# The last chunk's down projection in two token parts of 192 and 128 columns, with the final norm and the stores made per part

## The reference

```
def conv_ffn(h, buf, w_up, conv_w, conv_b, w_down):
    T = h.shape[1]
    z = h @ w_up
    a, v = z[..., :D_FF], z[..., D_FF:]
    ...
    hid = jax.nn.silu(conv) * v
    return hid @ w_down, ext[:, -(CONV_W - 1):]
...
    f, new_conv = conv_ffn(rmsnorm(x, norm_ffn_g), conv_buf, w_up, conv_w, conv_b, w_down)
    x = x + f
...
y = xf * lax.rsqrt(jnp.mean(xf * xf, axis=-1, keepdims=True) + EPS)
return (y * g.astype(jnp.float32)).astype(x.dtype)
```

## Time and profile before

| what | value |
|---|---|
| three runs | 2090.78, 2099.86, 2101.64 us, median 2099.86 |
| profiled execution | 2091.91 us, its span 2090.1 us |
| PE busy | 2017.1 us (97%), 13394 matmuls and as many weight loads |
| DVE, ACT busy | 1089.1 us (52%), 746.9 us (36%) |
| mean granted TensorE clock | 0.98 of full speed |

### The profile page before, as it was taken

How to read it: one execution, slowest core, us unless ns; L and a number is a source line. 1 busy time by engine, 2 the same in 40 slices (tenths; PEclk the granted TensorE clock), 3 DMA queues, 4 the chain that set the end, 5 groups by cost and what they waited for, 6 DMA issues and landing times.

```text
span 2090.1 us, 34134 instructions
## 1 busy us (share of the span) xinstructions
PE 2017.1 (97%) x13394; PEld 1958.9 (94%) x13394; DVE 1089.1 (52%) x1454; ACT 746.9 (36%) x810; POOL 55.6 (3%) x180
## 2 busy tenths in 40 slices
PE   7999999999999799999898999999999999999996
PEld 7999999999986688999898999999999999999996
DVE  6854344434336444145455656556556555555557
ACT  5356542332245443133243332333233233232332
POOL 0010000000000000000000000000000000000000
PEclk9999999999999899799999999999999999999998
DMA  6434444444450477334443434434443443433432
GB/s 226 151 140 147 159 142 159 140 155 147 145 217 21 150 244 259 134 141 154 161 157 128 150 139 155 148 141 153 148 153 140 150 151 140 149 148 144 158 143 98
DMA packets 58168, 318.16 MB, mean 152 GB/s; under 512 B 6466, under 2 KB 6658, under 8 KB 25090
## 3 DMA queue, kind: packets, MB, share of 16 engines
q1 hardware_dynamic: 57458, 313.15, 41.9%
q10 hardware_dynamic: 656, 4.27, 0.5%
HBM read 313.08 MB, written 4.32 MB: 152 GB/s over the span
## 4 chain that ended last, share of the span: by engine, by line
PE 93%; DVE 2%; ACT 1%; issue 1%; DMA 1%; SPq 0%; POOL 0%; ACTq 0%; DVEq 0%; POOLq 0%
PE ps L1118 93%; ACT w_hi L423 1%; DMA xT<-in_x 0%; PE ps L1375 0%; DVE x L1111 0%; PE ps L1288 0%; DVE x L707 0%; DVE w_lo L707 0%; DVE pool_ta L707 0%; DVE h_lo L783 0%; DMA c_raw<-in_cache 0%; PE ps L1308 0%; DVE norm_tmp L707 0%; DVE pool_tb L707 0%; POOL ql_lo L389 0%
## 5 line engine op out<-in xcount | busy, mean ns | idle before, releaser
L707 DVE TENSOR_TENSOR w_lo<-w_raw,w_hi 128x2048 fp32r<-128x2048 f32 (+1 forms) x267 | 609.7, 2284 | 496.2 <-ACT w_hi L423 495.9
L1118 PE MATMUL ps<-h_hi,w_hi 128*128 128x320 f32 x2512 | 746.6, 310 | 30.5 <-ACT w_hi L423 10.7
L423 ACT ACTIVATE w_hi<-w_raw 128x2048 fp32r<-128x2048 f32 (+1 forms) x267 | 508.3, 1905 | 700.6 <-PE ps L1118 694.3
L1118 PE MATMUL ps<-h_lo,w_hi 128*128 128x320 f32 x2512 | 744.5, 310 | 0.9 <-DVE h_lo L783 0.9
L1118 PEld LDWEIGHTS ps<-h_hi,w_hi 128*128 128x128 f32 x2512 | 475.5, 189 | 34.4 <-issue 13.4
L1118 PEld LDWEIGHTS ps<-h_lo,w_hi 128*128 128x128 f32 x2512 | 474.5, 189 | 1.9 <-DVE h_lo L783 1.6
L1118 PE MATMUL ps<-h_hi,w_lo 128*128 128x320 f32 x2512 | 393.6, 308 | 0.0
L1118 PEld LDWEIGHTS ps<-h_hi,w_lo 128*128 128x128 f32 x2512 | 374.9, 187 | 0.0
L1118 PE MATMUL ps<-hid_hi,w_hi 128*128 128x320 f32 x704 | 216.7, 308 | 0.0
L1118 PE MATMUL ps<-hid_lo,w_hi 128*128 128x320 f32 x704 | 216.6, 308 | 0.0
L1118 PE MATMUL ps<-hid_hi,w_lo 128*128 128x320 f32 x704 | 216.6, 308 | 0.0
(11 more groups left out here) (197 smaller groups left out, 1769.1 us busy)
## 6 DMA issues: line engine op xcount, KB each, us to landing
w_raw<-in_slabs SPq DMA_DIRECT2D x253, 1024.0 KB, 4.8
w_raw<-in_cache_t SPq DMA_DIRECT2D x64, 288.0 KB, 3.6
c_raw<-in_cache SPq DMA_DIRECT2D x64, 256.0 KB, 3.7
w_whole<-in_slabs SPq DMA_DIRECT2D x4, 1024.0 KB, 5.9
xT<-in_x SPq DMA_DIRECT2D x4, 640.0 KB, 8.4
x_again<-in_x ACTq DMA_DIRECT2D x1, 2560.0 KB, 11.4
out_y<-x SPq DMA_DIRECT2D x4, 640.0 KB, 2.9
w_raw<-in_slabs SPq DMA_DIRECT2D x2, 512.0 KB, 7.1
```

Of the source, the lines that this page charges most:

```text
L423: return nc.scalar.activation(out, in_, ACT.Copy)
L707: return nc.vector.tensor_tensor(out, a, b, op)
L1118: return nc.tensor.matmul(out, a, b, start=start, stop=stop, **kw)
```

## The change

The last chunk's down projection is taken out of `chunk` and written as `end_part(p, d)`. The tokens are cut in two parts, p = 0 with columns 0 to 191 and p = 1 with columns 192 to 319. First all four slabs are multiplied with part 0, then all four with part 1. For that all four split slabs have to stay: d = 0 and 1 in `w_hi`, `w_lo`, and d = 2 and 3 in new buffers `end_hi`, `end_lo` that lie where `h2_hi`, `h2_lo` lay. The normal loop now ends one chunk earlier on PE, and the up projection of the last chunk is written out.

```
+PARTS = ((0, 192), (192, T))
...
+        def end_tile(p, k):
+
+            d, n = k // 4, k % 4
+            width = PARTS[p][1] - PARTS[p][0]
+            high = d < 2 if p == 0 else d % 2 == 0
+            return ps[:, 4 * high + n, 0:width]
+
+        def end_sum_of(p):
+
+            return ps[:, 3 + p, 0:PARTS[p][1] - PARTS[p][0]]
...
+            for p, (c0, c1) in enumerate(PARTS):
+                for k in range(4):
+                    sp.wait_ge(y_step[p], k + 1)
+                    sp.dma_start(y[:, 4 * k:4 * k + 4, c0:c1], yg[:, 4 * k:4 * k + 4, c0:c1]).then_inc(out_sem, 16)
...
+            def end_tiles(p, k0, k1):
+
+                c0, c1 = PARTS[p]
+                for k in range(k0, k1):
+                    act.wait_ge(end_taken[p], k + 1)
+                    nc.scalar.activation(sq[:, k, c0:c1], x1[:, k, c0:c1], ACT.Square).then_inc(end_sq[p], 1)
+                    nc.scalar.activation(yg[:, k, c0:c1], x1[:, k, c0:c1], ACT.Copy, scale=col("g_fin", k)
+                                         ).then_inc(end_gain[p], 1)
...
+            def end_slab(d, g):
+
+                if d < 2:
+                    act.wait_ge(raw_full[d], 16 * ((raw_index(g) + 2) // 2 + 1))
+                    if d == 0:
+                        act.wait_ge(slab_used, G0["ffn"] + 12 * NCH - 4)
+                    copy(end_hi[d][:, :], raw[d]).then_inc(hi_ready, 1)
+                end_tiles(0, 4 * d, 4 * d + 4)
...
+            def end_add(p, d):
+
+                c0, c1 = PARTS[p]
+                for k in range(4 * d, 4 * d + 4):
+                    dve.wait_ge(end_done[p], k + 1)
+                    tt(x1[:, k, c0:c1], end_tile(p, k), x1[:, k, c0:c1], ALU.add).then_inc(end_taken[p], 1)
+
+            def end_squares(p, d):
+
+                c0, c1 = PARTS[p]
+                dve.wait_ge(end_sq[p], 4 * d + 4)
+                if d > 1:
+                    dve.wait_ge(end_added[p], d - 1)
+                tt(sq[:, 0:4, c0:c1], sq[:, 0:4, c0:c1], sq[:, 4 * d:4 * d + 4, c0:c1], ALU.add).then_inc(end_added[p], 1)
...
+            def end_scale(p, d):
+
+                c0, c1 = PARTS[p]
+                part = yg[:, 4 * d:4 * d + 4, c0:c1]
+                dve.wait_ge(end_gain[p], 4 * d + 4)
+                tt(part, part, rstd[:, None, c0:c1].to_broadcast([P, 4, c1 - c0]), ALU.mult).then_inc(y_step[p], 1)
+
+            def end_low(d):
+
+                dve.wait_ge(hi_ready, G0["ffn"] + 12 * NCH - 2 + d + 1 - NWHOLE)
+                tt(end_lo[d][:, :], raw[d], end_hi[d][:, :], ALU.subtract).then_inc(lo_ready, 1)
...
-            sum_squares(3, KD)
+            chunk(NCH - 1, last_chunk=True)
+
+            def end_part(p, d):
+
+                c0, c1 = PARTS[p]
+                whi, wlo = (w_hi[d], w_lo[d]) if d < 2 else (end_hi[d - 2], end_lo[d - 2])
...
+                order = ([(n, k) for k in range(FPC) for n in range(4)] if p == 0 and d == 0 else
+                         [(n, k) for n in range(4) for k in range(FPC)])
+                for n, k in order:
...
+                    if k == 0:
+                        if p == 0 and d % 2:
+                            pe.wait_ge(end_taken[0], 4 * (d - 1) + n + 1)
+                        if p and d < 2:
+                            pe.wait_ge(end_taken[0], 4 * (2 * d + 1) + n + 1)
+                        if p and d == 1 and n == 3:
+                            pe.wait_ge(end_norm[0], 1)
+                        if p and d >= 2:
+                            pe.wait_ge(end_taken[1], 4 * (d - 2) + n + 1)
+                    out = end_tile(p, 4 * d + n)
+                    w = 4 * n + k
+                    mm(out, blk(whi, w), hid_hi[:, k, c0:c1], k == 0, False)
+                    mm(out, blk(whi, w), hid_lo[:, k, c0:c1], False, False)
+                    last = mm(out, blk(wlo, w), hid_hi[:, k, c0:c1], False, k == FPC - 1)
+                    if k == FPC - 1:
+                        last.then_inc(end_done[p], 1)
...
+            for d in range(4):
+                end_part(0, d)
+            end_part(1, 0)
+            end_total(0)
+            for d in range(1, 4):
+                end_part(1, d)
+            end_total(1)
```

More of the change, by code:

```diff
@@ L202, in program @@
         cstate = sb("cstate", [P, FT, 1 + NB, CW - 1], at=b_reg + 12288)
+        end_hi = [sb(f"end_hi{s}", [P, SLAB], F32R, at=r1 + s * SLAB * 4) for s in range(2)]
+        end_lo = [sb(f"end_lo{s}", [P, SLAB], F32R, at=r1 + (2 + s) * SLAB * 4) for s in range(2)]
+        yg = sb("y_gain", [P, KD, T], at=ch_reg)
         ps = ctx.enter_context(nc.psum_tensor("ps", [P, 8, 512], F32))
@@ L681, in chunk @@
                         copy(hid_hi[:, f, :], hid32[:, f % 2, :]).then_inc(hd_hi, 1)
-                    if not (last_chunk and l >= 10):
+                    if last_chunk and l >= 8:
+                        end_slab(l - 8, g)
+                    else:
                         act.wait_ge(slab_used, g + 1)
@@ L685, in chunk @@
                         copy(w_hi[s][:, :], raw[s]).then_inc(hi_ready, 1)
[L686 to L689, removed]
                     if first_chunk and l == 0:
@@ L700, in _ @@
             chunk(NCH - 1, last_chunk=True)
-            root(3)
+            end_root(0)
+            end_tiles(1, 0, KD)
+            end_root(1)
         @block.vector
@@ new lines, in end_fold, with end_rsqrt @@
+            def end_fold(p):
+                c0, c1 = PARTS[p]
+                dve.wait_ge(end_added[p], 3)
+                tt(sq[:, 0:2, c0:c1], sq[:, 0:2, c0:c1], sq[:, 2:4, c0:c1], ALU.add).then_inc(end_added[p], 1)
+            def end_rsqrt(p):
+                c0, c1 = PARTS[p]
+                var, inv, tmp = nv[:, c0:c1], rstd[:, c0:c1], na[:, c0:c1]
+                dve.wait_ge(end_sum[p], 1)
+                nc.vector.tensor_scalar(var, end_sum_of(p), 1.0 / D, EPS, ALU.mult,
+                                        ALU.add).then_inc(end_norm[p], 1)
+                dve.wait_ge(end_norm[p], 2)
+                nc.vector.reciprocal(inv, inv).then_inc(end_norm[p], 1)
+                dve.wait_ge(end_norm[p], 3)
+                tt(tmp, inv, inv, ALU.mult).then_inc(end_norm[p], 1)
+                dve.wait_ge(end_norm[p], 4)
+                tt(tmp, tmp, var, ALU.mult).then_inc(end_norm[p], 1)
+                dve.wait_ge(end_norm[p], 5)
+                nc.vector.tensor_scalar(tmp, tmp, -0.5, 1.5, ALU.mult, ALU.add).then_inc(end_norm[p], 1)
+                dve.wait_ge(end_norm[p], 6)
+                tt(inv, inv, tmp, ALU.mult).then_inc(end_norm[p], 1)
+                dve.wait_ge(end_norm[p], 7)
@@ new lines, in end_chunk @@
+            def end_chunk():
+                end_low(0)
+                end_add(0, 0)
+                end_low(1)
+                end_add(0, 1)
+                end_squares(0, 1)
+                end_add(0, 2)
+                end_squares(0, 2)
+                end_add(0, 3)
+                end_squares(0, 3)
+                end_fold(0)
+                end_add(1, 0)
+                end_rsqrt(0)
+                end_add(1, 1)
+                end_scale(0, 0)
+                end_scale(0, 1)
+                end_squares(1, 1)
+                end_add(1, 2)
+                end_scale(0, 2)
+                end_squares(1, 2)
+                end_add(1, 3)
+                end_squares(1, 3)
+                end_fold(1)
+                end_scale(0, 3)
+                end_rsqrt(1)
+                for d in range(4):
+                    end_scale(1, d)
@@ L1039, in chunk @@
             def chunk(c, first_chunk=False, last_chunk=False):
-                for l in range(12):
+                for l in range(8 if last_chunk else 12):
                     s = l % 2
@@ L1072, in chunk @@
                             tt(x1[:, k, :], ps[:, bank, 0:T], x1[:, k, :], ALU.add).then_inc(dn_taken, 1)
[L1073 to L1078, removed]
+                    dve.wait_ge(hi_ready, g + (3 - NWHOLE))
+                    lo_of(s)
                     if first_chunk and l == 0:
@@ L1105, in _ @@
                 chunk(c)
-            acc_start(3)
             chunk(NCH - 1, last_chunk=True)
[L1109 to L1112, removed]
+            end_chunk()
         @block.tensor
@@ L1413, in _, with chunk @@
             group("w_o", lambda s: dense(s, m_hi, m_lo), before=lambda k: pe.wait_ge(mg_lo, k + 1))
-            def chunk(c, first_chunk=False):
+            def chunk(c, first_chunk=False, last_chunk=False):
                 for l in range(8):
@@ L1433, in chunk @@
                     pe.wait_ge(norm[2], 1)
+                if last_chunk:
+                    return
                 for d in range(4):
@@ new lines, in end_total @@
+            def end_total(p):
+                c0, c1 = PARTS[p]
+                pe.wait_ge(end_added[p], 4)
+                pe.wait_ge(end_taken[p], 16 if p == 0 else 9)
+                mm(end_sum_of(p), ones, sq[:, 0, c0:c1], True, False)
+                mm(end_sum_of(p), ones, sq[:, 1, c0:c1], False, True).then_inc(end_sum[p], 1)
```

(3 more changed lines are left out.)

26 lines of the change are left out of this document (20 added, 6 removed).

## The result

The changed kernel takes 2111.13 us (median of six runs, 2105.13 to 2114.19), the kernel before 2099.95 us beside it (six runs, 2090.78 to 2101.64). The ratio is 1.0059 with a 95% interval of 1.0039 to 1.0078: slower by about 12 us. The profiled execution took 2105.13 us against 2091.91.

A forecast was written before the change was run, and what follows sets the result against it. PE was taken as the bound, busy 2017.1 of 2090.1 us. Terms 14.5 + 3.2 + 1.6 + 0.7 - 8.1 = +11.9 us on the median 2099.9 gave 2111.8 us, range 2101 to 2133, the forecast's own 2108 to 2117.

The forecast's parts named there:

- step 3: PE's clock after its idle wait in the last down projection: 0.50 for 3.4 us, costing +1.6 us, bounds none to 3.2.
- Step 1: PE's last down projection: 384 narrow matmuls bound by weight loads, 0.112 us each, 43.0 us against 28.5, so +14.5 us.
- Rival B: PE's narrow matmuls cost only their columns, spacing under 0.108 us; sum +2 us, 2102; 10 in 100.
- rival D: PE's narrow float32r matmuls handled like float32, two records each; +73 us, given as 2185; 10 in 100.
- Step 2: Part 0, d = 1: PE waits for banks 4 to 7 until DVE's split and first addition end, about 2050.1; +3.2 us.
- Later tiles don't wait: Part 0, after the first bank wait: PE takes 1.34 us a tile, an addition 0.35, d = 3's split wanted at 2063 only.
- first three signs: PE's timeline: narrow matmuls 0.112 us apart; about 3 us idle near 2047 to 2050; clock 0.50 for 3.4 us, then 1.00.
- Step 4: Part 0's sum over the partitions inside PE's stream: four float32 records of 192 columns, +0.7 us, bounds 0.45 and 1.3.
- Step 5: Tail after PE's last matmul: 8.4 us to the last product, 3.5 for the store; 11.9 against 20.0 us, so -8.1.
- Rival C: The clock stays down in part 1's narrow matmuls, at 1.2 GHz; +31 us, 2131, half way +21; 18 in 100.
- Rival E: The bank wait before part 0's d = 1 is hidden after all and the clock keeps up; +7 us, 2107; 5 in 100.
- rival A: The forecast itself, PE's stream bound by weight loads; from +8 to +17 us with its bounds; 57 in 100.

The follow-up runs named there:

- half the weights' columns: The first experiment's kernel with 128x64 instead of 128x128 weight blocks in the last down projection, half the output features left out; stage 50.9 us, stream 38.1, one run.
- the halves paired: The first experiment's kernel with high and low activations side by side, one matmul by w_hi making both products; stage 56.3 us, ratio 1.0046 to the kernel before.
- the run with the additions first: The changed kernel, banks as they are, with DVE making d = 0's additions before the split of d = 2; stage 61.0 us against 61.7, one run.
- The kernel with one part: The changed kernel with one part of 320 columns instead of two, banks as in the first experiment; stage 49.2 us, ratio 1.0017 to the kernel before.
- the first experiment: Also the banks experiment: the changed kernel with part 0's d = 1 in banks 0 to 3, avoiding the wait; stage 56.7 us against 61.7, ratio 1.0041 to before.

## Why the prediction was right

The forecast was 2111.8 us, and the sign, the size and four of the five terms were borne out; the size of step 3 was not. Term by term, of the stage in the profile:

| step | forecast | measured |
|---|---|---|
| 1, PE's stream | +14.5 | +14.6 |
| 2, wait for banks | +3.2 | +3.1 |
| 3, clock behind it | +1.6 | +2.8 |
| 4, part 0's sum in the stream | +0.7 | +0.6 |
| 5, tail | -8.1 | -8.0 |
| sum | +11.9 | +13.1 |

**Step 1** held, and for the reason given: 192 and 128 columns both stand 0.112 us apart, 384 x 0.112 = 43.0 us and 0.2 for the last one's end, against 28.6. The experiments with half the weights' columns and with the halves paired show the cause. Rival B would have needed a spacing under 0.108 and falls, rival D (two records a matmul) too. The pair gap of the Trainium skill (TensorE: Matmul & The Clock Gate, Back-to-back issue gap), some 81 ns at 128 columns, does not hold here either: the rows show 0.11 us.

**Step 2** held to 0.1 us. DVE took the split of d = 2 at 2047.42, and PE went on at 2050.12 (2050.1 forecast). The banks experiment shows that the wait hangs on the banks, and the run with the additions first (0.86 instead of 3.06 us) that its length comes from the split ahead of them. One sentence of the step was right only under cover: "Later tiles don't wait". In the change none does, but the run with the additions first has a wait of 2.65 us at d = 3. I had compared the time of the split of d = 3 with PE's need and left out what stands behind that split on DVE ahead of the additions of d = 2. The delay of step 2 hid it.

**Step 3** had the right mechanism and too small a size. I took the 3.4 us of the earlier trace rows as the length of the slow stretch; it lasted 6.8 us, 5.9 of them behind the wait, so the loss is 28 x 0.101 = 2.8 us, near the upper bound of 3.2. The prediction calls itself wrong if one of its first three signs is off, and the third, 0.50 for 3.4 us, is off in its length, though not in its place or in the 1.00 of part 1. Two experiments without the long idle time kept the clock at 1.00 in the stream. Why the slow stretch is 3.4 us in one run and about twice that in another is open.

**Step 4**: the four records push the next matmul 0.57 us back, from 2074.40 to 2074.97.

**Step 5** held: 8.3 us from PE's last matmul to the last product (8.4 forecast), then 3.7 us for the store (3.5 forecast). For the first 1.5 us behind the last product the DMA engines are busy all the time and move 281 GB/s; in the kernel before they move 356 GB/s with a share of 0.88, while the last products run. The kernel with one part compares better, since its DMA engines are as busy: 410 GB/s with a share of 1.01 (2088 to 2090). The pieces of 512 bytes go slower than those of 5120, but the last store takes only some 0.3 us longer than before, 3.7 against 3.4.
```profile
2099.50:2101.00 1.50, 0.00 (x0) 0.00 (x0) 0.05 (x1) 0.00 (x0) 0.00 (x0) 0.50 1.02 281
2101.00:2103.30 2.30, 0.00 (x0) 0.00 (x0) 0.00 (x0) 0.00 (x0) 0.00 (x0) 0.50 0.61 172
```
Of the kernel before:
```profile
2085.00:2086.70 1.70, 0.00 (x0) 0.00 (x0) 1.68 (x4) 0.00 (x0) 0.00 (x0) 0.50 0.88 356
```

**The sum** is 1.2 us too low, all of it from step 3. That the median of the runs, 2111.13, lies within 0.7 us of the forecast is partly luck: the profiled executions are 13.2 us apart, the medians 11.2. **Rival C** described what 64 columns do and was wrong of the change: part 1 with 128 columns ran at 1.00 for its 22 us. **Rival E** (the wait hidden) did not happen. No wait for instructions arose from the unrolled chunk. Two numbers of the rivals were added up wrongly: rival D's +73 on the median of 2099.9 is 2173, not 2185, and rival A's own bounds reach +18.4, not +17, so the forecast's own range should have ended near 2118.

So where the expected gain went: the tail did shrink by 8.0 us, and PE's stream took back 14.6 us of it and more, because each part pays the weight loads again. With the banks of the first experiment the change still loses 8.1 us. None of the variants run beats the kernel before by more than can be measured.

## What to carry to other kernels

Before a stream of matmuls is cut into narrower ones to shorten what follows, compare the width with the spacing that a weight load alone sets: here 128 x 128 weights cost 0.112 us, which 320 columns (0.147) cover and 192 do not, so that every weight load made twice costs 2 x 0.112 - 0.147 = 0.077 us, 192 times here. Count these against the tail; only the part of the tail that is really hidden behind the narrow matmuls comes back, and a smaller split hides less. When a wait is removed, look up the next reuse of the same banks in the order of the engine that frees them, since the first delay may have hidden a second.

## What the runs showed of the hardware that was not expected

The granted clock fell to 0.50 within a stretch of matmuls that had no idle time at all, with 64 columns each 0.11 us apart, and not with 128 columns at the same distance. Idle times of 3.06 and 2.65 us in this stage were both followed by the low clock: in the first case it fell 0.9 us before PE went on and stayed at 0.50 for 6.8 us, in the second it fell 1.7 us after PE had gone on and stayed for 3.4 us. The idle times of 3.28 us (half the weights' columns) and 3.38 us (paired) were followed by it too; those of 0.86, 1.69 and 1.66 us were not. With the weight load halved, float32r matmuls cost 0.46 ns a column down to 128 columns. The stores with pieces of 512 bytes kept the DMA engines at a share of 1.02 with 281 GB/s; those with 5120 bytes moved 356 GB/s at a share of 0.88 in the kernel before and 410 at 1.01 in the kernel with one part.
